# Attention stream of a two-block network: query halves copied out of their banks and projected in separate stages, four probability buffers, exponentials issued ahead of evictions

## The reference, cut to what matters

```
cq  = rms_norm(cq) * q_norm          # 256 features
q   = (cq @ w_q_up)                  # 8 heads x (64 + 32), the last 32 rotated by position
k   = concat(rms_norm(ckv) @ w_k, rotated kr)
s   = einsum('bqhd,bkhd->bhqk', q, k) * scale
p   = softmax(s, axis=-1)
o   = einsum('bhqk,bkhd->bqhd', p, v)
y   = o * silu(d_gate)
```

## Time and profile before

| | us |
|---|---|
| median of 3 executions | 4160.15 |
| lowest and highest | 4159.56, 4166.65 |
| the profiled execution, its own time | 4164.0 |
| its span (first to last instruction) | 4162.2 |
| attention phase, about | 3435 to 3884 of the span |
| mean granted TensorE clock over the span | 0.897 |

### The profile page before, as it was taken

The page is one execution under the profiler, slowest core; times in us unless marked ns, Lnnn a source line. Parts: engine busy times, 40 slices in busy tenths (PEclk is TensorE's granted clock), DMA queues, the critical chain, the costliest instruction groups (busy, mean ns, idle before and its releaser), DMA issues. The chain is left out here.

```text
span 4162.2 us, 46766 instructions
## 1 busy us (share of the span) xinstructions
PE 3413.1 (82%) x18746; PEld 2959.0 (71%) x18746; DVE 1960.9 (47%) x2600; ACT 896.6 (22%) x1009; POOL 100.0 (2%) x85
## 2 busy tenths in 40 slices
PE   4999999988067599898998984898395886998886
PEld 4999999978055499898897883787273773555454
DVE  5555555652878234464363453212923214666223
ACT  3222222222210311111111113100113104444211
POOL 0000000000000000000000000000000000222000
PEclk9999999999576699999999997999697997999998
DMA  2222222233611433212212114222332211000222
GB/s 95 87 78 87 87 87 87 77 108 116 127 19 27 135 106 115 86 45 81 86 45 100 62 58 167 89 81 107 116 129 107 96 75 65 1 1 1 92 84 118
DMA packets 112071, 346.74 MB, mean 83 GB/s; under 512 B 13888, under 2 KB 31680, under 8 KB 111552
## 3 DMA queue, kind: packets, MB, share of 16 engines
q1 hardware_dynamic: 111936, 344.93, 24.9%
HBM read 247.74 MB, written 97.14 MB: 83 GB/s over the span
## 5 line engine op out<-in xcount | busy, mean ns | idle before, releaser
L736 PE MATMUL mixer_in_dense<-mix_z_high,mixer_in_whigh 128*128 128x348 f32 x1344 | 444.4, 331 | 11.0 <-DVE mixer_in_wlow L747 11.0
L736 PE MATMUL mixer_in_dense<-mix_z_high,mixer_in_wlow 128*128 128x348 f32 x1344 | 437.3, 325 | 0.0
L736 PE MATMUL mixer_in_dense<-mix_z_low,mixer_in_whigh 128*128 128x348 f32 x1344 | 436.5, 325 | 0.0
L138 PE MATMUL up_psum<-first_operand_b_high,up_whigh 128*128 128x342 f32 x1056 | 340.6, 322 | 22.7 <-DVE up_wlow L262 22.7
L138 PE MATMUL up_psum<-first_operand_b_low,up_whigh 128*128 128x342 f32 x1056 | 339.2, 321 | 0.0
L138 PE MATMUL up_psum<-first_operand_b_high,up_wlow 128*128 128x342 f32 x1056 | 339.0, 321 | 0.0
L736 PEld LDWEIGHTS mixer_in_dense<-mix_z_high,mixer_in_whigh 128*128 128x128 f32 x1344 | 258.2, 192 | 13.3 <-issue 12.0
L736 PEld LDWEIGHTS mixer_in_dense<-mix_z_high,mixer_in_wlow 128*128 128x128 f32 x1344 | 257.4, 192 | 0.8
L736 PEld LDWEIGHTS mixer_in_dense<-mix_z_low,mixer_in_whigh 128*128 128x128 f32 x1344 | 257.0, 191 | 0.0
L138 PE MATMUL ab_in_psum<-abx_operand_high,ab_in_whigh 128*128 128x512 f32 (+1 forms) x480 | 171.0, 356 | 61.6 <-DVE ab_in_wlow L262 61.6
L138 PEld LDWEIGHTS up_psum<-first_operand_b_high,up_whigh 128*128 128x128 f32 x1056 | 201.4, 191 | 24.5 <-DVE up_wlow L262 24.5
(11 more groups left out here) (496 smaller groups left out, 7263.9 us busy)
## 6 DMA issues: line engine op xcount, KB each, us to landing
mixer_in_wstage<-w_in SPq DMA_DIRECT2D x56, 512.0 KB, 4.7
mixer_in_mod_w<-w_mod SPq DMA_DIRECT2D x64, 384.0 KB, 3.6
first_weights<-w_up SPq DMA_DIRECT2D x44, 512.0 KB, 3.3
abz<-ab_in_out SPq DMA_DIRECT2D x20, 640.0 KB, 3.0
p<-mixer_in_out SPq DMA_DIRECT2D x24, 528.0 KB, 2.9
down_side<-h SPq DMA_DIRECT2D x24, 512.0 KB, 4.3
h<-down_out SPq DMA_DIRECT2D x24, 512.0 KB, 2.9
ab_in_wstage<-ab_w_in SPq DMA_DIRECT2D x20, 512.0 KB, 4.6
```

What stands on the lines that cost most here:

```text
L138: mm = pe.matmul(o, a[:, k * P:(k + 1) * P], x[:, k, first + c0:first + c0 + w], start=(k == 0 and t == 0), stop=(k == kt - 1 and t == 2))
L736: mm = pe.matmul(pd[s % 2][:, 0:W], a[n % 2][:, P * m:P * (m + 1)], z[x][:, m, W * b:W * (b + 1)], start=m == 0 and i == 0, stop=m == DT - ...
```

## The change

Four things, all in `attend`:

1. *Queries.* ScalarE copies a half's whole bank to a buffer `rq` and the plain rows to the high part, then releases the bank (it was VectorE). VectorE's rotation and low parts read `rq`. There is one `rq`, so ScalarE's next copy waits for VectorE's last read. The halves are made in two stages: half 0 after a head's first stage; half 1 with key piece 2 after the second; key pieces 0 and 1 after the third.
2. *Turned probabilities.* Units are regrouped: 0 and 1 are block a's key tiles 0 to 7, 2 is tiles 8 and 9 of both blocks, 3 and 4 are block b's tiles 0 to 7. VectorE evicts units 0 to 3 and ScalarE unit 4. Value pairs come in up to two groups, after units 0 and 1 and after units 2 and 3.
3. *Probabilities* lie in four buffers, and ScalarE's exponentials come ahead of its eviction.
4. *Preamble.* Silu of the gates comes after the roots and the key copies; both Ln come before both Exp; GpSimd waits for the gates.

```diff
-        return ((("q", h + 1, 0), ("q", h + 1, 1)), (("k", h + 1, 0), ("k", h + 1, 1)), (("k", h + 1, 2),), ())[j]
+        return ((("q", h + 1, 0),), (("q", h + 1, 1), ("k", h + 1, 2)), (("k", h + 1, 0), ("k", h + 1, 1)), ())[j]
...
-    by_act = ring.count([n for n in names if n[0] == "v" and n[1] % 2 == 0 or n[0] == "t" and n[2] < 2])
+    by_act = ring.count([n for n in names if n[0] == "v" and n[1] % 2 == 0 or n[0] == "t" and n[2] == 4 or n[0] == "q"])
...
+    def unit(i):
+
+        if i == 2:
+            return [(ab, k) for ab in range(2) for k in (8, 9)]
+        return [(i // 3, 4 * (i % 3) + k) for k in range(4)]
...
-        pr = [ph.sb(f"probs{j}", (P, T2)) for j in range(3)]
+        pr = [ph.sb(f"probs{j}", (P, T2)) for j in range(4)]
...
+                    for g, (ab, k) in enumerate(unit(i)):
+                        if i in (0, 2) and g % 2 == 0:
+                            pe.wait_ge(normal, 2 * s + ab + 1)
...
-                    for n in turned_at(s):
+                    turns = turned_at(s)
+                    for n in turns[0:2]:
                         turn_probs(n)
-                        if n[2] % 2 and H is not None:
-                            value_sums(H, pairs[n[2] // 2:n[2] // 2 + 1])
-                    if s <= NS and H is not None:
+                    if H is not None:
+                        value_sums(H, pairs[0:2])
+                    for n in turns[2:4]:
+                        turn_probs(n)
+                    if H is not None:
                         value_sums(H, pairs[2:])
-                    elif H is not None:
-                        value_sums(H, pairs)
+                    for n in turns[4:]:
+                        turn_probs(n)
...
+                        if h or b:
+                            act.wait_ge(lows, HL.at(h if b else h - 1, "rope0" if b else "rope1"))
+                        act.activation(rq[:, :], o[:, :], ACT.Copy).then_inc(raw, 1)
                         act.activation(qh[h % 2][0:NOPE, at], o[0:NOPE, :], ACT.Copy).then_inc(highs, 1)
+                        act.wait_ge(raw, 2 * h + b + 1)
+                        act.wait_ge(highs, HL.at(h, f"q{b}"))
+                        act.sem_inc(act_freed, 1)
                         act.wait_ge(turned, 2 * h + b + 1)
-                        act.activation(qh[h % 2][A, at], r1[A, :], ACT.Copy).then_inc(highs, 1)
+                        act.activation(qh[h % 2][A, at], rq[A, :], ACT.Copy).then_inc(highs, 1)
...
-                act.wait_ge(gates_in, 64)
-                for m in range(4):
-                    act.activation(dg[:, m, :], dg[:, m, :], ACT.Silu)
                 act.wait_ge(summed, 1)
-                inverse_root(act, root[:, :], pS[:, 0:SEQ], c["eps"][:, 0:1], 1.0 / QL, rooted)
-                inverse_root(act, rk[:, :], pS[:, SEQ:SEQ + T2], c["eps"][:, 0:1], 1.0 / KVL, rooted, 2)
+                act.activation(root[:, :], pS[:, 0:SEQ], ACT.Ln, bias=c["eps"][:, 0:1], scale=1.0 / QL).then_inc(rooted, 1)
...
+                act.wait_ge(gates_in, 64)
+                for m in range(4):
+                    act.activation(dg[:, m, :], dg[:, m, :], ACT.Silu).then_inc(gates_made, 1)
...
-                    for n in turned_at(s):
-                        if n in by_act:
-                            move(n)
                     if s < NS:
                         for ab in range(2):
                             i = 2 * s + ab
                             act.wait_ge(biased, s + 1)
-                            if i >= 3:
-                                act.wait_ge(full, ring[("t", (i - 3) // 2, 4)] + 1)
+                            if i >= 4:
+                                act.wait_ge(full, ring[("t", (i - 4) // 2, 4)] + 1)
...
+                    for n in turned_at(s):
+                        if n in by_act:
+                            move(n)
...
                     if kind == "q":
                         at = slice(HALF * b, HALF * (b + 1))
-                        dve.wait_ge(full, ring[n] + 1)
+                        o = rq
+                        dve.wait_ge(raw, 2 * h + b + 1)
...
                         dve.wait_ge(lows, HL.at(h, "q0") + 2 * b)
-                        dve.sem_inc(dve_freed, 1)
```

More of the change, by code:

```diff
@@ L1831, in made_at @@
             return ()
-        return ((("q", h + 1, 0), ("q", h + 1, 1)), (("k", h + 1, 0), ("k", h + 1, 1)), (("k", h + 1, 2),), ())[j]
+        return ((("q", h + 1, 0),), (("q", h + 1, 1), ("k", h + 1, 2)), (("k", h + 1, 0), ("k", h + 1, 1)), ())[j]
     def turned_at(s):
         return tuple(("t", s - 1, i) for i in range(5)) if 1 <= s <= NS else ()
-    first = tuple(("q", 0, b) for b in range(2)) + tuple(("k", 0, b) for b in range(3))
+    first = tuple(("q", 0, b) for b in range(2)) + tuple(("k", 0, b) for b in (2, 0, 1))
     values = tuple(("v", b) for b in range(NKT))
@@ L1860, in attend @@
         kh, kl = ([ph.sb(f"{n}{j}", (P, T2), F32R) for j in range(2)] for n in ("key_high", "key_low"))
-        r1, r2 = ph.sb("turned_cos", (P, HALF)), ph.sb("turned_sin", (P, HALF))
-        pr = [ph.sb(f"probs{j}", (P, T2)) for j in range(3)]
+        rq, r2 = ph.sb("query", (P, HALF)), ph.sb("turned_sin", (P, HALF))
+        raw = ph.sem("query_moved")
+        pr = [ph.sb(f"probs{j}", (P, T2)) for j in range(4)]
         PT = [ph.sb(f"turned_probs{j}", (P, NKT, HALF)) for j in range(2)]
@@ L1937, in pair_scores @@
                     if j == 0:
-                        pe.wait_ge(lows, HL.at(h, "k2"))
+                        pe.wait_ge(lows, HL.at(h, "k1"))
                         if h == 0:
@@ L1954, in turn_probs @@
                     o = wait_free(pe, n)
[L1955 to L1962, removed]
+                    for g, (ab, k) in enumerate(unit(i)):
+                        if i in (0, 2) and g % 2 == 0:
+                            pe.wait_ge(normal, 2 * s + ab + 1)
+                        c0 = P * k if ab == 0 else (CTX + P * k if k < 8 else P * (k - 8))
+                        mm = pe.transpose(o[:, P * g:P * g + P], pr[(2 * s + ab) % 4][:, c0:c0 + P], c["ident"][:, :])
                     mm.then_inc(full, 1)
@@ L1973, in value_sums @@
                             last = ("t", 2 * H + 1, 4)
-                            pe.wait_ge(dve_freed, by_dve[last])
-                            pe.wait_ge(act_freed, by_act[("t", 2 * H + 1, 1)])
+                            pe.wait_ge(act_freed, by_act[last])
+                            pe.wait_ge(dve_freed, by_dve[("t", 2 * H + 1, 3)])
                         for g in range(2):
@@ L2023, in move @@
                         H = s // 2
-                        if s % 2 == 0 and i == 0 and H >= 2:
+                        if s % 2 == 0 and H >= 2:
                             act.wait_ge(y_full, H - 1)
-                        act.activation(PT[H % 2][:, 2 * i:2 * i + 2, 256 * (s % 2):256 * (s % 2) + 256],
-                                       o[:, :].rearrange("p (a b) -> p a b", a=2), ACT.Copy).then_inc(act_freed, 1)
+                        dst, src = unit_rows(o, PT[H % 2], n)
+                        act.activation(dst, src, ACT.Copy).then_inc(act_freed, 1)
                 def high(n):
@@ L2100, in move @@
                         H = s // 2
-                        if s % 2 == 0 and i == 2 and H >= 2:
+                        if s % 2 == 0 and i == 0 and H >= 2:
                             dve.wait_ge(y_full, H - 1)
-                        dve.tensor_copy(PT[H % 2][:, 2 * i:2 * i + 2, 256 * (s % 2):256 * (s % 2) + 256],
-                                        o[:, :].rearrange("p (a b) -> p a b", a=2)).then_inc(dve_freed, 1)
+                        dst, src = unit_rows(o, PT[H % 2], n)
+                        dve.tensor_copy(dst, src).then_inc(dve_freed, 1)
                 def low(n):
@@ L2202, in _ @@
                         at = slice(HALF * (H % 2), HALF * (H % 2 + 1))
+                        pool.wait_ge(gates_made, 4)
                         pool.wait_ge(y_added, H + 1)
```

30 lines of the change are left out of this document (22 added, 8 removed).

## The result

Over 20 executions of each kernel the changed one took 4168.92 us in the median (4162.24 to 4177.14) and the kernel before 4161.39: a ratio of 1.0019 with a 95% interval of 1.0012 to 1.0026, 5 to 11 us slower. The profiled execution took 4166.86 us for a span of 4165.0.

A forecast was written before the change was run, and what follows sets the result against it. The prediction took VectorE's chain on the query halves, not the bank, to end the query step. Loop +3.6, preamble -6.1, tail -2 and clock +12 gave +7.5 us, so 4168 us, range 4145 to 4185.

The forecast's parts named there:

- Preamble and tail: Before and after the loop: earlier roots, -6.1 us (-8.2 to -3); earlier last normalising, -2 us (-3.5 to 0).
- The steps at full clock: Attention loop: plain-head steps of 13.7, 13.0, 10.65, 8.35 us, gated head 51.0; loop +3.6 us (-4 to +11).
- The first head: First head of the loop: first step 18.9 us, then 13.0, 10.2, 8.3; 50.4 in all, before 47.08.
- The clock: TensorE in the loop: 9 or 10 half-speed spells behind new gaps, 1.3 us each, +12 us (3 to 22).
- Before it did so once a head ...; now twice: Query steps: VectorE idles from its reciprocal until the half arrives, some 2.7 us, in two stages a head.
- there is nothing to win below that: Steps without projections: 8.25 or 8.8 us with the new evictions, against TensorE's own work of 7.8 and 8.7.
- The rule against the rows: VectorE's work on a half: rows show bank and memory operands alike, 0.69 and 0.68 us, despite the skill's copy-out rule.
- (c): Rival, VectorE's query work: copied operands run faster, five operations a half at half time, -24 us, 4136; chance 0.03.
- (a): Rival, TensorE's clock: no clock loss, gaps shorter or spells beside VectorE's work; -4.5 us, 4156; chance 0.27.
- (b): Rival, query bank was the bound: half 0 waits ready for VectorE, saving 38 us, near 4118, half 4137; chance 0.10.
- (d): Rival, TensorE's clock: more clock loss, a spell after every gap, +22 us, 4178 to 4182; chance 0.12.

The follow-up runs named there:

- with the gaps filled: Changed kernel with value pairs repeated in TensorE's gaps of heads 1 to 6; loop 370.06 us against the changed kernel's 376.46.
- the link of the new units, evictions and order: From the kernel before with split halves and four buffers to the changed kernel without the bank copy, new preamble included; loop 346.31 to 367.27 us.
- the early version: Kernel before with new preamble, four buffers, ScalarE evicting units 0, 1, 4, halves projected before unit 4, read from bank, keys in third step; 4127.01 us, ratio 0.9924.

## Why the prediction was right

The time came out at 4168.9 where 4168 was said, and the interval of the ratio lies above 1, so it is slower, which had a chance of 0.42 against 0.40 for no change. These two were as good as equal, and 7.5 us is less than the 8.3 that the prediction took as the least that can be told. Of what was said for the time, not all holds.

*Preamble and tail.* -6.1 was said, 6.3 measured from the first square to the first mark; the roots end 5.9 us behind the sums (3454.54 to 3460.43) where it was 14.3, the 8.2 us worked out and a little more, and the copy's wait for its one buffer and the third key piece take their parts. The tail gave 3.3, not 2: the term was a little small, within its bounds.

*The steps at full clock.* Said 13.7, 13.0, 10.65, 8.35; with the gaps filled 13.39, 12.89, 10.79, 8.25, and a gated head 50.7 against 51.0. Half 0 reaches VectorE at R+6.2, said 6.1. This part of the sum is right to 0.3 us a step. The first head is the exception: 53.6 and not 50.4. Its first step is 20.56 and not 18.9: with the values made just before, the half is copied at the very moment when GpSimd normalises, and two operations take 1.65 and 1.71 us instead of 0.69. That term was missing. Its later steps (13.64, 11.10) had two half-clock spells.

*The clock.* Said +12, nine or ten spells of 1.3. Nine spells came in the six heads that the filling covers, and eight of them cost 7.1 us, 0.9 each: the number was right, the price was a third too high. The loop's +13.6 against the 15.6 that its two terms gave is therefore partly luck: 4.9 too much for the clock stands against 3.2 too little for the first head, and the rest is 0.3 off. The new spells do not come on top of the old ones: the clock is at half for 34.1 us of the loop before and for 40.9 of the changed one. Before's own spells went with the split (6.8 us at half), and the later links brought new ones.

*The sum and the total.* In the two profiled executions the phase is 4.0 us longer (-6.3 + 13.6 - 3.3), while the medians differ by 7.5 (5 to 11). The first square of the phase stood at different times in the traces of this case (3437.48 to 3447.57 us), with the same work ahead of it, and what lies outside the phase takes 3716 to 3727 us in them. Where the other 3.5 us come from is not shown by one pair of traces and stays open. So the sum of +7.5 meets the medians to a tenth by luck; in the traces it was 3.5 us too much.

*The attribution.* The time held, but one reading did not: "Before it did so once a head ...; now twice". I put the loss on the split. The split by itself wins 12.8 us on the kernel before, and undoing it in the changed one loses 6, the clock having its part in both. The loss lies in the link of the new units, evictions and order, +21.0 us, where "evictions" was costed at nothing lost ("there is nothing to win below that"). For steps without projections that is right (8.25, said 8.25). What it costs elsewhere is seen in the second step: the half stands on TensorE behind units that wait for VectorE's copies behind R, and its matmuls start at R+2.9 instead of R+1.4. Of the 3.74 us that VectorE then waits, 1.35 are the half-clock spell, 0.65 the copy, 1.4 this later start, and 0.3 are there with the old evictions too. The key pieces of the third step are held back in the same way (+1.3). In the first step the new order brings the half earlier, not later. This accounts for the 4.9 us of the plain heads; how the other 16 us of the link, in the first and the gated heads, divide among its parts and the clock is not shown. I had worked out the half's start about correctly (R+3.05), but had not compared it with what the old order would have given a split half.

*The rule against the rows.* Rows 3 showed no difference between a bank operand and a memory operand, and the tier table of the Trainium skill ("VectorE: DVE Perf Modes") agreed. Both are true with GpSimd silent. Beside its normalising the copied operand is the slow one, up to 1.74 against 0.69: rival (c) did not come, and where the two engines meet its sign is reversed. In the changed kernel they meet in the first head alone, so this is part of the first head's term and not of the others. One row of before could have told it: the rotation's sum in the first head took 1.80 us there, beside GpSimd, and I did not look for it.

*The rivals.* (a), no clock loss, falls by the filled gaps. (b), a half that waits ready for VectorE, did not come in this change; the early version comes near it (VectorE waits 0.5 to 0.6 us in a plain head). (b) was said to be worth up to 38 us, and that version gained 35, with the preamble and the buffers in it. (c)'s 4136 left out the -4.5 of the other terms that (b)'s has; with it, it is 4132. (d) did not come.

## What to carry to other kernels

Before a stage is split or moved, write down for its product where it stands in the producer's queue and what the entries ahead of it wait for: here much of what a good split had won was lost because the second half and the key pieces stood behind copies that the same change had put on the late side of the maxima. Change parts one at a time: the split and the buffers were gains (12.8 and 3.8 us), the new order of units and evictions and the copy were losses (about 19.5 and 9.2), and only the chain of single steps shows that. An operand copied out of a bank is not free for its reader either: it moves the reader to a memory that a third engine uses, which cost nothing where that engine was done and 0.5 to 0.7 us a step where it was not.

## What the runs showed of the hardware that I had not expected

VectorE's two-operand operations on 512 columns take 0.68 us with both operands in memory, and 0.80 to 1.82 us where they run into GpSimd multiplying a 1280-column tile in memory; with one operand in a PSUM bank they stay at 0.68 to 0.70 throughout. Putting the first product back into its bank (VectorE writing there) took the rotation's sum from a median of 1.24 to 0.69 in all sixteen instances. GpSimd can pay as well: two normalisings take 3.08 us instead of 2.65 where VectorE's operation came in between them, as in the row at 3566.82. The rows look like one engine waiting out the other: at 3567.61 VectorE's operation takes 1.09 us, of which 0.68 is its own time and 0.4 the rest of GpSimd's first tile; at 3568.72 it takes 1.72, its own 0.68 and 1.04 of the second. The Trainium skill states this ("SBUF — State Buffer", section Who interferes with whom): an operation of VectorE with two inputs in memory and one of GpSimd that reads memory exclude each other, and the later one waits the other out. The trace agrees. I had not brought it to bear on the copy, which is the part of the change that it speaks against; in the changed kernel the two meet in the first head alone, in the split kernel with the copy in every one that makes a half.

The nine half-clock spells in the six heads of the changed kernel last 3.4 us each, and each lies behind a gap of TensorE of 1.7 us or more; filling the gaps with repeated work removed eight. What a spell costs depends on the step that it falls into. The fourth step of a gated head takes 7.05 us without one (new preamble alone), 8.60 with one of 3.4 us (before) and 10.07 with one of 6.8 us (new preamble alone, a later head): 1.5 and 3.0 us, where those of the changed kernel cost 0.9 on average.
